# A modulation's matrix-vector products, moved from TensorE to VectorE

## The reference, cut to what matters

```python
c_act = jax.nn.silu(c)
for i in range(DEPTH):
    mod = (c_act @ mod_w[i] + mod_b[i]).reshape(B, N_SUBLAYERS, 3, D)
    shift, scale, gate = mod[:, :, 0], mod[:, :, 1], mod[:, :, 2]
    h = modulate(rms_norm(x, norm_g[i, 0]), shift[:, 0], scale[:, 0])
    x = x + 0.5 * gate[:, 0, None, :] * swiglu(h, ...)          # feed-forward
    ...                                                         # attention, then a second feed-forward, in the same form
```

## Time and profile before

| | |
|---|---|
| runs | 2389.92 us (2389.13 to 2393.08) |
| profiled execution | 2388.34 us, its span 2387.0 us |
| TensorE, products | 2287.9 us, 96% |
| VectorE | 1315.5 us, 55% |
| ScalarE | 1155.0 us, 48% |
| granted TensorE clock, mean | 0.99 |
| DMA | 439.78 MB, mean 184 GB/s |

### The profile page before, as it was taken

One profiled execution on the slowest core, in us unless ns is written; L12 is line 12 of the kernel. 1 busy time (PEld: TensorE's weight loads), 2 busy tenths in 40 slices (PEclk: granted clock), 3 DMA queues, 4 the chain that ended last, 5 costly groups with the idle time before them and its releaser, 6 DMA issues.

```text
span 2387.0 us, 38790 instructions
## 1 busy us (share of the span) xinstructions
PE 2287.9 (96%) x17008; PEld 2093.1 (88%) x17008; DVE 1315.5 (55%) x1763; ACT 1155.0 (48%) x1348; POOL 59.8 (3%) x72
## 2 busy tenths in 40 slices
PE   6999998999999999899899999999999999999998
PEld 3999777999899978677799997899999988989998
DVE  2543554544554466456455445556786544666873
ACT  4443555543544354544454345654555446436553
POOL 2000000000000000000000011000000020000000
PEclk9999999999999999999999999999999999999999
DMA  8767562676576657246165555433655464445550
GB/s 308 263 232 266 204 228 66 212 247 242 165 263 210 237 184 257 98 159 212 36 213 188 184 196 170 157 127 124 212 177 195 134 215 129 154 142 174 180 195 18
DMA packets 273592, 439.78 MB, mean 184 GB/s; under 512 B 10656, under 2 KB 147152, under 8 KB 273296
## 3 DMA queue, kind: packets, MB, share of 16 engines
q1 hardware_dynamic: 270880, 429.07, 53.3%
q0 software_dynamic: 2256, 7.12, 0.9%
q10 hardware_dynamic: 288, 1.11, 0.1%
HBM read 436.22 MB, written 1.05 MB: 183 GB/s over the span
## 4 chain that ended last, share of the span: by engine, by line
PE 90%; ACT 4%; DVE 3%; DMA 1%; issue 1%; SPq 0%; POOL 0%; ACTq 0%; POOLq 0%; DVEq 0%
PE ps L1266 89%; DVE wlo L1675 1%; ACT whi L1488 1%; ACT PT L1488 1%; PE ps L1454 1%; PE ps L1366 1%; DMA raw<-in_mod_w 1%; ACT L1488 0%; ACT xhi L1488 0%; DMA raw<-in_fox_w_in 0%; ACT S L1488 0%; SPq L1255 0%; DVE x L1707 0%; DVE xlo L1753 0%; DMA raw<-in_ffn_w_down 0%
## 5 line engine op out<-in xcount | busy, mean ns | idle before, releaser
L1675 DVE TENSOR_TENSOR wlo<-raw,whi 128x2048 fp32r<-128x2048 f32 x339 | 769.0, 2274 | 592.3 <-ACT whi L1488 592.1
L1488 ACT ACTIVATE whi<-raw 128x2048 fp32r<-128x2048 f32 x339 | 640.8, 1895 | 424.1 <-PE ps L1266 388.2
L1266 PE MATMUL ps<-xhi,whi 128*128 128x256 f32 x2888 | 735.0, 286 | 14.1 <-ACT xhi L1488 11.3
L1266 PE MATMUL ps<-xhi,wlo 128*128 128x256 f32 x2888 | 729.3, 284 | 0.0
L1266 PEld LDWEIGHTS ps<-xhi,whi 128*128 128x128 f32 x2888 | 557.1, 193 | 28.2 <-issue 27.4
L1266 PEld LDWEIGHTS ps<-xhi,wlo 128*128 128x128 f32 x2888 | 557.1, 193 | 0.3
L1266 PE MATMUL ps<-xlo,whi 128*128 128x256 f32 x2888 | 472.0, 284 | 3.6 <-DVE xlo L1893 3.4
L1266 PEld LDWEIGHTS ps<-xlo,whi 128*128 128x128 f32 x2888 | 402.3, 193 | 4.4 <-DVE xlo L1893 3.8
L1266 PE MATMUL ps<-hhi,whi 128*128 128x256 f32 x1056 | 298.9, 283 | 0.9 <-DVE modc L1688 0.9
L1266 PE MATMUL ps<-hlo,whi 128*128 128x256 f32 x1056 | 298.4, 283 | 0.0
L1266 PE MATMUL ps<-hhi,wlo 128*128 128x256 f32 x1056 | 297.6, 282 | 0.0
(11 more groups left out here) (220 smaller groups left out, 2043.3 us busy)
## 6 DMA issues: line engine op xcount, KB each, us to landing
raw<-in_mod_w SPq DMA_DIRECT2D x72, 1024.0 KB, 9.1
raw<-in_w_in SPq DMA_DIRECT2D x52, 1024.0 KB, 5.1
raw<-in_ffn_w_gate SPq DMA_DIRECT2D x88, 512.0 KB, 6.1
raw<-in_ffn_w_up SPq DMA_DIRECT2D x88, 512.0 KB, 7.5
raw<-in_ffn_w_down SPq DMA_DIRECT2D x44, 1024.0 KB, 6.6
raw<-in_w_up SPq DMA_DIRECT2D x88, 512.0 KB, 4.7
raw<-in_dil_w_in SPq DMA_DIRECT2D x36, 1024.0 KB, 6.4
raw<-in_w_down SPq DMA_DIRECT2D x22, 1024.0 KB, 4.9
```

What stands on the lines that cost most here:

```text
L1266: return nc.tensor.matmul(o, lhs, rhs, start=start, stop=stop, skip_group_check=True)
L1488: return nc.scalar.activation(o, i, func, **kw)
L1675: V.tensor_tensor(wlo[:, s["c"], 0:s["n"]], raw[:, s["slot"], 0:s["n"]], whi[:, s["c"], 0:s["n"]].bitcast(F32), ALU.subtract).then_inc(sem ...
```

## The change

32 of the 36 units, all but the first four, take another way. `mod_beside` plans them: VectorE multiplies each of the eight 128 x 512 chunks by its number of `c` per partition and sums them in `mrow` (`mod_acc`); later (`mod_sum`) TensorE multiplies each quarter of `mrow` by a column of ones, which adds up the partitions, and VectorE adds the bias. The norm's unit is planned ahead of the norm instead of inside it. A unit's sum waits until more than two further `run_mods` have gone by, or the next unit, or the norm or tail that needs it.

```diff
+MOD_LAG = 2
+    def run_mods(self, upto=None):
+        for m in self.mod_turns:
+            m[2] += 1
+        while self.mod_turns and (self.mod_turns[0][2] > MOD_LAG or upto and self.mod_turns[0][:2] <= list(upto)):
+            self.mod_turns.pop(0)[3]()
+    def mod_beside(self, i, u):
+        while self.mod_turns:
+            self.mod_turns.pop(0)[3]()
+        acc_free = self.mod_row_free
+        for h in range(2):
+            pc = self.take()
+            toks = [self.ev("dve", "mod_acc") for _ in range(4)]
+            self.add("mod_acc", h=h, slot=pc["slot"], landed=pc["landed"], acc_free=acc_free, acc=toks)
+            self.used(pc, toks[-1])
+        self.mod_turns.append([i, u, 0, lambda: self.mod_sum(i, u, toks[-1])])
...
-                self.mod_unit(i, u, s.get("bank", D3) - u % 2, CONV if self.in_stage else 0)
+                if self.in_stage:
+                    self.mod_beside(i, u)
+                else:
+                    self.mod_unit(i, u, D3 - u % 2, 0)
...
-                self.norm(i, s["s"], buf, tail.tok, (lambda: self.mod_unit(*md, D3 - md[1] % 2, 1)) if md else None)
+                if md:
+                    self.mod_beside(*md)
+                self.norm(i, s["s"], buf, tail.tok)
...
+                elif k == "mod_sum":                                   # TensorE
+                    q.wait_ge(s["mod_acc"])
+                    q.wait_ge(s["bank_free"])
+                    q.wait_ge(("const_set", 5))
+                    for m in range(4):
+                        ins = mm(ps[:, s["bank"], m:m + 1], mrow[:, m * P:(m + 1) * P], epst[:, 2:3], m == 0, True)
+                    ins.then_inc(sem["mod_turned"])
...
+                elif k == "mod_acc":                                   # VectorE
+                    q.wait_ge(("c_silu", 1))
+                    q.wait_ge(s["acc_free"])
+                    q.wait_ge(s["landed"])
+                    v = raw[:, s["slot"], :].rearrange("p (k n) -> p k n", k=4)
+                    for kk in range(4):
+                        c = csil[:, 4 * s["h"] + kk, 0:1]
+                        if s["h"] == 0 and kk == 0:
+                            V.tensor_scalar(mrow[:, :], v[:, kk, :], c, None, ALU.mult).then_inc(sem["mod_acc"])
+                        else:
+                            V.scalar_tensor_tensor(out=mrow[:, :], in0=v[:, kk, :], scalar=c, in1=mrow[:, :], op0=ALU.mult,
+                                                   op1=ALU.add).then_inc(sem["mod_acc"])
+                        q.wait_ge(s["acc"][kk])
```

More of the change, by code:

```diff
@@ L29 @@
     "c_in", "mod_in", "ident_in", "x_in", "small_in", "late_in", "out_st",
-    "const_set", "c_silu", "w_hi", "w_lo", "piece", "mod_mm", "mod_row", "mod_turned", "mod_col",
+    "const_set", "c_silu", "w_hi", "w_lo", "piece", "mod_mm", "mod_row", "mod_turned", "mod_col", "mod_acc",
     "square", "stat", "diag", "sqrt", "recip", "rows", "scaled", "x_hi", "x_mod", "x_lo", "resid",
@@ L61, in __init__ @@
         self.mod_row_free = None
+        self.mod_bank = D2
         self.mod_ready = {}
@@ L149, in used, with run_turns @@
         self.use += 1
-    def run_turns(self, mod_only=False):
-        while self.turns and not mod_only:
+    def run_turns(self):
+        while self.turns:
             self.turns.pop(0)()
-        while self.mod_turns:
-            self.mod_turns.pop(0)()
+        self.run_mods()
+    def run_mods(self, upto=None):
[3 more added lines that the diff above has]
+            self.mod_turns.pop(0)[3]()
     def run_beside(self):
@@ L218, in mod_unit @@
             self.used(pc, tok)
-        self.run_turns(True)
+        self.run_mods()
         row = self.ev("act", "mod_row")
@@ L222, in mod_unit @@
         self.free[bank] = row
-        self.mod_turns.append(lambda: self.mod_turn(i, u, bank, row))
+        self.mod_turns.append([i, u, MOD_LAG, lambda: self.mod_turn(i, u, bank, row)])
     def mod_turn(self, i, u, bank, row):
@@ L232, in mod_turn, with mod_columns @@
         self.free[bank] = col
+        self.mod_columns(s, i, u)
+    def mod_columns(self, s, i, u):
         tok = s["mod_bias"] = self.ev("dve", "mod_col")
@@ L238, in mod_turn, with mod_sum @@
             self.mod_ready[(i, sub, kind)] = tok
+    def mod_beside(self, i, u):
[8 more added lines that the diff above has]
+        self.mod_turns.append([i, u, 0, lambda: self.mod_sum(i, u, toks[-1])])
+    def mod_sum(self, i, u, acc):
+        bank = self.mod_bank
+        bank_free = self.free[bank]
+        summed = self.mod_row_free = self.ev("pe", "mod_turned")
+        s = self.add("mod_sum", i=i, u=u, bank=bank, bank_free=bank_free, mod_acc=acc, mod_turned=summed,
+                     shift_read=self.shift_read.get(u // 2))
+        self.mod_columns(s, i, u)
+        self.free[bank] = s["mod_bias"]
     def square(self, m, after):
@@ L252, in stat, with rstd @@
         return tok
-    def rstd(self, stat, eps, src=G0, dst=G1, between=None):
+    def rstd(self, stat, eps, src=G0, dst=G1):
         diag = self.ev("dve", "diag")
@@ L261, in rstd @@
         self.sq_free[0] = summed
-        if between:
-            between()
         rows = self.ev("pe", "rows")
@@ L266, in rstd, with norm @@
         return rows
-    def norm(self, i, s, buf, stat, between=None):
-        rows = self.rstd(stat, 0, between=between)
+    def norm(self, i, s, buf, stat):
+        rows = self.rstd(stat, 0)
+        self.mod_bank = D2
         if (i, s) == (0, 0):
@@ L272, in norm @@
         self.pair = 0
+        self.run_mods((i, 6 * s + 3))
         am, bm = self.mod_ready[(i, s, 0)], self.mod_ready[(i, s, 1)]
@@ L328, in down @@
         bank_free = []
+        self.mod_bank = G3
         if q == 0:
@@ L892, in ffn @@
                     for m in at[11 + q]:
-                        step("mod", i=m[0], u=m[1], bank=G3)
+                        step("mod", i=m[0], u=m[1])
         def mix(i):
@@ L1035, in lay_out @@
                 if s["q"] == FB // 2 - 1:
+                    self.run_mods((i, 12 * s["j"] + 5))
                     tail = Tail(self, self.update("gate", i, 2 * s["j"]), "split" if (i, s["j"]) == (1, 1) else "square")
@@ L1048, in lay_out @@
             elif k == "mix_out":
+                self.mod_bank = G3
                 if u == 1:
+                    self.run_mods((i, 11))
                     tail = Tail(self, self.update("gate", i, 1), "square")
@@ L1670, in dve_program @@
             V.memset(epst[:, 1:2], 1e-5).then_inc(sem["const_set"])
+            V.memset(epst[:, 2:3], 1.0).then_inc(sem["const_set"])
             for s in plan.steps:
@@ L1687, in dve_program @@
                     c0 = mod[:, 4 * u:4 * u + 4]
[L1688 to L1691, removed]
+                    b0 = modb[:, i, 4 * u:4 * u + 4]
+                    if k == "mod_turn":
+                        V.tensor_reduce(c0, ps[:, s["bank"], :].rearrange("p (m g n) -> p m g n", m=4, g=4)[:, :, :, 0], AX.X,
+                                        ALU.add).then_inc(sem["mod_col"])
+                        q.wait_ge(s["mod_col"])
+                        V.tensor_tensor(c0, c0, b0, ALU.add).then_inc(sem["mod_col"])
+                    else:
+                        V.tensor_tensor(c0, ps[:, s["bank"], 0:4], b0, ALU.add).then_inc(sem["mod_col"])
                     if u % 2 and kind:
```

2 lines of the change are left out of this document (1 added, 1 removed).

## The result

| | before | after |
|---|---|---|
| median of the runs | 2390.49 us (2389.13 to 2393.08, 4 runs) | 2488.91 us (2484.53 to 2491.2, 4 runs) |
| profiled span | 2387.0 us | 2489.9 us |
| granted TensorE clock, mean | 0.99 | 0.96 |

The ratio is 1.0408, with a 95% interval of 1.039 to 1.0426: slower, by 98.4 us of the medians. The prediction was 2475 (2420 to 2515). The profiled execution of the kernel after was the slowest of its four, so the two spans differ by more, 102.9 us.

The account below looks back on a forecast made before the run. TensorE, busy 96%, was taken as the bound, except at norms, where VectorE and ScalarE are the path. Terms -42 +2.5 +64 +21 +31 +13.5 +7.5 gave +97.5, less 12: +85, 2475 us by the median (65%), range 2420 to 2515.

Parts of the forecast that it names:

- 27 units between pieces: Units between weight pieces, where TensorE is the bound: each gains 1.56 us, 42 us in all.
- five norms, their sums, their clock: At norms, sums, slot transfers and conversions delay the diagonal, 64 us; products no longer hidden, 2.5; cold clock behind pauses, 2.6 each.
- fox, with one cold restart: Fox projection: TensorE waits 24 us for unit 13's sums, later pieces come late; 31 us, bounds 12 and 40, plus clock.
- first feed-forward, with one restart: Down steps: units 9 and 10 two pieces apart, conversion and sums late; 13.5 us, bounds 4 and 18, plus clock.
- dilated attention, with one restart: First bias operation of the dilated attention stands behind 5.8 us of sums; 7.5 us with the gain counted elsewhere, plus clock.
- given back by DMA: Long chains in fox and down steps were laid end to end; idling DMA gives some back, 12 us taken off.
- TensorE, per unit: Between pieces, product and transposes of 2.46 us give way to four one-column fp32 products of 0.9: gain 1.56 us.
- VectorE: Eight operations of 0.725 us, 5.8 per unit; 186 us more, busy 55% to 63%, no price in itself.
- rival 2: Queue only: VectorE's sums delay norms and attention, slots and transfers don't; +35 us, 2425; chance 20%.
- Rival 1: TensorE's time is simply gained, with no wait for the sums; 40 us less, 2350; chance 5%.
- The clock: Pauses over 6 us, eight of them, each leave TensorE at half clock, 2.6 us: 21 us, between 0 and 30.
- the cover of the gate-up steps: Gate-up steps: later conversions and slot transfers, landing about 5 us after issue, stay covered with 2 to 3 us to spare.

Follow-up runs that it names:

- experiment 1: Kernel after with the norms' five units back on TensorE between statistics and diagonal, the other 27 on VectorE: 2419.03 us, ratio 1.0118 to before.
- 3: Kernel after with the four units between fox's projections back on TensorE, the rest unchanged: 2464.31 us, ratio 1.0307 to before.
- 8: Kernel after with only 15 units on VectorE, none in first feed-forward, fox or norms; norm's transposes put off again: 2360.79 us, ratio 0.9878 to before.
- Experiment 2: Kernel after with the norm's unit planned with a look-ahead of one conversion instead of three: 2460.44 us, ratio 1.0288 to before.
- experiment 11: Kernel after with 34 to 74 constant products keeping TensorE busy in the norms' pauses, nearly to their end: 2481.89 us, ratio 1.0386 to before.
- experiment 5: Kernel after with only 18 spaced units on VectorE; both kinds of unit shared a PSUM bank: 2391.57 us, ratio 0.9999 to before.
- experiment 6: Kernel after with 26 to 60 constant products keeping TensorE busy in the norms' pauses, ending early: 2487.78 us, ratio 1.0404 to before.

## Why the prediction was right, and where it was not

Each term against what the runs show. The plain sum of the prediction was 97.5, less 12.

| term | predicted | measured | from |
|---|---|---|---|
| 27 units between pieces | -42 | -43 | period of gate-up units |
| five norms, their sums, their clock | 64 + 2.5 + 13 | 66 | 1 against after |
| fox, with one cold restart | 31 + 2.6 | 31.8 | 3: 25.4, and the 6.4 of gain that goes with it |
| first feed-forward, with one restart | 13.5 + 2.6 | 31.7 | 1 against before: 20.6, and 7 x 1.59 |
| dilated attention, with one restart | 7.5 + 2.6 | 9.3 | 8 against 1: 7.75, and 1.59 |
| ahead of the first row | 0 | 4 | windows |
| given back by DMA | -12 | 0 | what is left over |
| sum | 85 | 100 | medians: 98.4, spans: 102.9 |

The measured column has some play. Since experiment 1 has its transposes early, the norms' 66 is up to 5.3 us low (by the first product's 1.0 to 1.2 us at each norm), and the first feed-forward and the dilated attention up to 1.2 and 1.0 high. The 4 us ahead of the first row are no effect of the change, as said below.

*TensorE, per unit: right.* Two sums a period apart in the kernel after start at 553.93 and 589.36; 35.43 against 37.02 is 1.59 us, 1.56 was predicted. A warm sum takes 0.95 (0.9 taken).

*VectorE: right in sum, wrong in parts.* The unit takes 6.0 us (5.8): the accumulating operation is slower than the tensor-by-tensor row it was priced by, 752 against 685 ns, and the first is faster, 481. On that one I weighed a rule of the Trainium skill ("VectorE: DVE Perf Modes", Mode 2x_2P: fp32 tensor_scalar within SBUF runs at two elements a cycle) and said that the row did not agree. It does: 512 elements in 481 ns and 128 in 287 make 0.505 ns per element, half of the 1.03 of the tensor-by-tensor rows, and a fixed part of 0.22. The mistake was to subtract a fixed part borrowed from another operation from a single row; by the rule the first operation takes 0.27 us less than by 1.03 ns per element, and it takes 0.27 less than the accumulating one and 0.20 less than the row of 685.

*Norms: right, by the order of the queue itself.* The pauses are 16.90, 17.12 and 17.10 us at the feed-forward norms, 11.78 at the dilated one and 8.17 at fox. The last 1.5 us of each lie between the diagonal and the rows; without them VectorE's queue took 15.4, 15.7, 15.6, 10.3 and 6.7, where 15 to 17, 10 and 6.3 were predicted, the landing of 5.2 against 5. Experiment 2 shows the part of the conversions and the slot (28.5 us; 30 expected), and refutes rival 2, in which slots don't matter. Rival 1 had no wait of TensorE for the sums; the 29.8 us ahead of sums and these pauses refute it.

*The clock: the mechanism and the size at the norms were right, a place was missing.* It is 0.50 behind the pauses in the kernel after:

```profile
502.00:504.70 2.70, 1.22 (x4) 0.93 (x5) 0.92 (x3) 0.73 (x3) 0.00 (x0) 0.50 1.00 317
504.70:507.00 2.30, 2.27 (x11) 2.30 (x12) 1.51 (x4) 2.30 (x6) 0.00 (x0) 0.50 1.08 354
```

A restart behind a norm costs 2.2 us by experiment 11, 2.6 were predicted. What I priced at nothing is the clock behind the short waits in a stage where TensorE is dense. In the windows of the kernel after around the two late sums of the down steps:

```profile
203.00:210.00 7.00, 6.91 (x35) 6.94 (x36) 5.15 (x7) 2.41 (x2) 0.00 (x0) 0.55 0.36 129
210.00:222.00 12.00, 8.53 (x72) 8.32 (x70) 5.09 (x6) 1.92 (x1) 0.00 (x0) 1.00 0.26 87
222.00:231.00 9.00, 8.27 (x44) 8.27 (x45) 0.76 (x2) 1.92 (x1) 0.00 (x0) 0.62 0.79 304
```

Each wait of 4 us is followed by some 20 to 25 products 0.213 apart instead of 0.12, 1.9 and 2.4 us, and the sum in front of them takes 1.84 and 1.67 instead of 0.95.

*Fox: right.* TensorE waited 23.43 us for the sums of unit 13 (24 predicted), through the steps that the prediction names: slot, head norm of k, a conversion, sums. VectorE's rows of the kernel after:

```profile
329.66 2.29 DVE L1723 TENSOR_TENSOR wlo<-raw,whi 128x2048 fp32r<-128x2048 f32 x1 [9.73 <-ACT whi L1535]
...
336.22 2.28 DVE L1723 TENSOR_TENSOR wlo<-raw,whi 128x2048 fp32r<-128x2048 f32 x1
338.42 0.48 DVE L1738 TENSOR_SCALAR mrow<-raw,csil 128x512 f32<-128x512 f32 x1
338.93 5.48 DVE L1740 SCALAR_TENSOR_TENSOR mrow<-raw,csil,mrow 128x512 f32<-128x512 f32 x7
```

*Dilated attention: right.* The first bias operation of the attention stands behind a conversion and the sums, and the products behind it waited 11.12 us, against 1.81 before. In the kernel after:

```profile
1057.10 5.48 DVE L1740 SCALAR_TENSOR_TENSOR mrow<-raw,csil,mrow 128x512 f32<-128x512 f32 x7
1062.61 0.56 DVE L1840 CUSTOM_DVE_ANT_0 S<-ps,dmask 128x384 f32<-128x384 f32 x1
```

*First feed-forward: the step that failed.* The prediction had the gate-up steps covered, "with 2 to 3 us to spare", and only the down steps late. In the kernel after:

```profile
85.60 1.91 ACT L1535 ACTIVATE whi<-raw 128x2048 fp32r<-128x2048 f32 x1 [5.66 <-DMA raw<-in_ffn_w_up]
...
87.54 2.29 DVE L1723 TENSOR_TENSOR wlo<-raw,whi 128x2048 fp32r<-128x2048 f32 x1 [6.88 <-ACT whi L1535]
...
89.98 0.55 PE L1306 MATMUL ps<-xhi,whi 128*128 128x256 f32 x1 [2.95 <-DVE wlo L1723]
```

The sums that give the slots back end at 76.35. SyncE's queue of the kernel after in that stretch:

```profile
73.22 3.52 SPq L1295 DMA_DIRECT2D raw<-in_mod_w  x2
76.79 0.51 SPq L1295 DMA_DIRECT2D raw<-in_ffn_w_gate  x1
77.34 0.81 SPq L1295 DMA_DIRECT2D raw<-in_ffn_w_up  x1
```

Between two units of this stage lie mostly two steps with four pieces; with the unit's own two that is six, the number of slots, so a unit's slots go to the next unit's weights. These, 2 MB in a stretch in which DMA moved 309 GB/s (window 73 to 86), stand ahead of the piece that TensorE needs: issued from 76.79 on, it is there at 85.60, 8.8 us later and not the 5 that the cover was reckoned with (the median of the transfers of `in_ffn_w_up` is 8.4). I had looked at a single transfer and at neither its size nor what goes ahead of it. The units stand closer here, too: their sums come at 86.09, 114.54 and 141.17, against one in 35.4 us in the stages (0,1) and (1,0), whose gate-up steps show no such waits. Four of them make 8.1 us (1.48, 2.95, 1.09, 2.57), the two at the down steps 8.3 (13.5 predicted). In experiment 1, without the norm's unit, TensorE's idle time in the stage is 24.1 us against 3.6 before, 20.5 more. Its busy time is 217.01 against 216.87, although the seven units' 11.1 us of products are gone, so 11.3 us are busy time that should not be there. Most of that is the clock. Read in windows of 0.5 us, TensorE is busy for 27 us of this stage at half clock, against 5.4 before; at 0.213 us apart for 0.12 the difference is worth 9.5 us, where the prediction had one restart of 2.6. Together that is 30 of 31.7, and the rest is open. So two terms of the sum failed here: the cover of the gate-up steps, and the clock behind short waits, put at nothing.

*The 12 us taken off.* Nothing shows them. DMA was less busy (61% against 67% in the first feed-forward), but the other terms add up to the loss without any of it given back; no run isolates this. The plain sum, 97.5, was nearer to the 98.4 than the forecast was; it came so near in part by errors of opposite sign (the norms with their clock 8 to 13 too high, the first feed-forward some 15 too low), which is luck. The 4 us ahead of the first row lie in work that neither the change nor any experiment touches. The first row of the windows starts at 42.92 us before and 46.86 after, at 46.47 in experiment 5 and between 42.37 and 44.50 in the other ten. Half clock makes the difference: the sixth group of eight products takes 1.94 us in the kernel after and in experiment 5, and 1.06 before and in 8. So it is the spread of single executions, and not a cost of the change.

## What to carry to other kernels

Work moved from a busy engine to an idle one is paid for in the queue it is put into: write down what stands behind it there, and which buffer is now given back by the other engine and later, before counting the gain. Here the same edit is worth +4.1% in all 32 places and -1.2% in the 15 where VectorE's queue and the slots had room. Where a cover is reckoned with a transfer's landing time, take it from the stage in question; and price a short stall of a dense TensorE with the products at half clock behind it.

## What the runs showed of the hardware

- An fp32 scalar_tensor_tensor of 128x512 within SBUF takes 752 ns, a tensor_tensor 685, a tensor_scalar 481 (start to start 0.787 for the first, in a chain of its own results).
- A product of a 128x128 fp32 weight with one column costs 0.12 us per record (eight in 0.95), at half clock 0.23 (1.87).
- TensorE's clock behind a pause. In experiment 6 TensorE was kept busy, paused 2.4 to 3.9 us, took a norm's rows (at four of the five norms in 0.71 or 0.72 us, so at full clock), waited 1.24 us, and the products behind ran at 0.50, at all five. In experiment 11 it paused 0.6 to 0.8 us, with the same 1.24 behind the rows, and the clock stayed at 1.00 at four norms and fell to 0.50 at one. The length of a wait alone does not tell: in the kernel after, one of 1.48 us ahead of 62.99 left the clock at 1.00, and one of 1.09 ahead of 116.58, behind a unit's sum, was followed by 0.50.
